# The second memory's keys and values as products of two fp32r parts, with the low parts made on GpSimd

## The chip, the cores and the metric

The kernel runs on one core of one Trainium2 chip. The metric is the device time of one execution in microseconds (us). Three runs of the kernel before gave 2437.41 us (median), from 2435.37 to 2440.38. TensorE is called PE in the rows, VectorE DVE, ScalarE ACT, GpSimd POOL, and SyncE, which issues most transfers, SP.

## The reference, cut to what matters

256 tokens of width 1024 pass through a three-layer stack (two layers of the first block, one of the second), in fp32 throughout. The change touches layer 1 of the first block, in which a Conformer convolution is followed by a cross attention to a memory of 256 rows:

```
def conformer_conv(xn, pw1_w, pw1_b, dw_w, dw_b, ln_g, ln_b, pw2_w, pw2_b):
    a, g = jnp.split(xn @ pw1_w + pw1_b, 2, axis=-1)
    h = a * jax.nn.sigmoid(g)
    h = depthwise_conv(h, dw_w) + dw_b           # 31 taps, 1024 channels
    h = jax.nn.silu(layernorm(h, ln_g, ln_b))
    return h @ pw2_w + pw2_b

def cross_attn(xn, mem, norm_mem, wq, wkv, wo):
    q = (xn @ wq).reshape(b, s, 4, 256)
    k, v = jnp.split(rmsnorm(mem, norm_mem) @ wkv, 2, axis=-1)
    ...
```

The keys and values depend on the memory alone and not on the tokens, so `rmsnorm(mem) @ wkv` (256x1024 by 1024x2048) can be computed at any time before the attention. There are three memories, one for each layer: A, B and C. The second one, B, is that of layer 1.

## The kernel before

**Units and panels.** The dense products are cut into units of 512 output columns (`UNITS`, lines 107 to 158). A unit's weights are one panel of 128 x 8 x 512 floats (2 MB), which SP loads into one of three slots of a ring (line 458). A unit is computed in one of two ways (`project`, line 603):

- *As parts.* The panel is taken in two halves of 128x2048. ScalarE rounds a half to fp32r into `w_high` (`highs`, line 1231), then VectorE subtracts that from the source and writes the rest, also in fp32r, to `w_low` (`lows`, line 1595). There are three buffers of each (`SPLITS`). The inputs are split likewise: ScalarE writes `XT_high` (`columns_high`, line 1220), VectorE `XT_low` (`columns_low`, line 1586). TensorE computes each product as three matmuls, high by high, low by high and high by low (`product`, lines 679 to 681).
- *Plain.* TensorE multiplies the fp32 panel itself (lines 617 and 622). ScalarE and VectorE each copy half of the fp32 input columns to `XT` (`columns`, lines 1206 and 1571).

Nearly all units go as parts. Plain are the four of memory B (`Bk0`, `Bk1`: keys; `Bv0`, `Bv1`: values) and `mix0`, `mix1`, `pw2_0`, `pw2_1`.

**Counters.** `parts_high` counts the halves that ScalarE has rounded, `parts_split` those whose low part is written, `parts_read` those that TensorE has read. A half waits for the one three places before it to be read. SP loads a panel when the panel three places before it is released: by `parts_split` for a unit as parts, and when TensorE is done with it for a plain one.

**The order around the change** is written out by hand on each engine. TensorE computes the gates and values of the convolution's gated input (`gate0`, `value0`, `gate1`, `value1`, as parts), transposes the normalised memory (line 666), computes `Bk0`, `Bk1`, `Bv0`, `Bv1`, does the convolution of 2 of the 8 blocks of 128 channels with 62 diagonal matrices (line 841), sums the channels for the layer norm (lines 846 and 850), computes `pw2_0` and `pw2_1` (line 622) and goes on to the attention. ScalarE evicts the four units (lines 1242 and 1237), and after the last it makes the 62 diagonals in six buffers (line 1383). VectorE, once it has copied its half of the memory's columns, does the convolution of the other 6 blocks: 6 instructions of line 1853 and 180 of line 1855, 31 rounds of 6, each `CO = HC * weight + CO` over 128x256 floats, with `HC`, `CO` and the weight in SBUF. The first channel sums wait for both parts of the convolution. GpSimd issues transfers only: after it has asked for memory B (line 537) it waits until the bias row of `pw2` has been used (line 1868).

**The same thing once before.** Memory A in layer 0 has the same four units, as parts already: its highs and columns are ScalarE's, its lows are VectorE's, between other work.

Of the kernel before, what the change touches and what calls it, by code (L numbers as in the profile page):

```python
# [14 lines left out]
F32 = mybir.dt.float32  # L15
F32R = mybir.dt.float32r
I32 = mybir.dt.int32
ALU = mybir.AluOpType
# [95 lines left out]


def _memory_units(tag, layer, wk, wv, v0):
    src = "memory" if tag == "B" else "x"
    for j in range(2):
        _unit(f"{tag}k{j}", wk, j * PANEL, PANEL, True, src, layer)
    for j in range(2):  # L120
        _unit(f"{tag}v{j}", wv, v0 + j * PANEL, PANEL, False, src, layer)
# [75 lines left out]
def program(nc, ins, const_in, out):  # L197
    ctx = ExitStack()
    with ctx:
# [5 lines left out]
        def S(name):  # L205
            if name not in sems:
                sems[name] = ctx.enter_context(nc.semaphore(name))
            return sems[name]

        ring = sb("ring", [P, 7, HALF])  # L210
        w_high = sb("w_high", [P, SPLITS, HALF], F32R)
        w_low = sb("w_low", [P, SPLITS, HALF], F32R)
        parts = sb("parts", [P, 3 * KC * P], F32R)
# [5 lines left out]
        XS = sb("XS", [P, HALVES, D])  # L219
# [154 lines left out]
        def half_source(q):  # L374


            i, kind, half, n = pieces_split[q]
            if kind == "rows":
                return ring[:, 2 * slot(i), :]
            if kind == "features":  # L380
                return slot_kn(slot(i))[:, 4 * half:4 * half + 4, 0:n]
            if q in range(ffn_at, ffn_at + 3 * FFN_TURNS):
                return slot_kn(slot(i)).rearrange("p k (g n) -> p k g n", g=2)[:, :, :, half * P:(half + 1) * P]
            return slot_kn(slot(i))[:, :, half * T:(half + 1) * T]

        def half_tile(q, parts):

            t, (_, kind, _, n) = parts[:, q % SPLITS, :], pieces_split[q]
            if kind == "rows":
                return t  # L390
            if kind == "features":
                return t.rearrange("p (k n) -> p k n", n=PANEL)[:, :, 0:n]
            if q in range(ffn_at, ffn_at + 3 * FFN_TURNS):
                return t.rearrange("p (k g n) -> p k g n", g=2, n=P)
            return t.rearrange("p (k n) -> p k n", n=T)

        def halves_to(name, more=0):

            return split_at[UNIT[name]] + 2 + more
# [123 lines left out]
        def _(pool):  # L523
# [11 lines left out]
            def memory(turns, name):  # L535
                pool.wait_ge(S("turned"), 4 * turns)
                pool.dma_start(XS[:, :, :], ins[name][0].rearrange("(a p) d -> p a d", p=P)).then_inc(S("memory_loaded"), 16)
# [3 lines left out]
            def row(b, src):  # L541

                if loads[b]:
                    pool.wait_ge(S(f"brow{b}_used"), loads[b])
                loads[b] += 1
                pool.dma_start(brow[:, b, :], src).then_inc(S(f"brow{b}_loaded"), 16)
# [27 lines left out]
            pool.wait_ge(S("pool_mixed"), 1)  # L574
            row(0, ins["od_pw2_b"][0].partition_broadcast(P))
            memory(5, "mem")
            row(0, ins["od_norm_moe"][0].partition_broadcast(P))
            row(0, ins["ln_in_g_2"].partition_broadcast(P))
            expert_rows(1, XS, "xs_ready", 8)
# [19 lines left out]
        def _(pe):  # L599
# [54 lines left out]
            def turn(src, ready, n, parts=True):  # L654

                pe.wait_ge(S(ready), n)
                if seen["act"]:
                    pe.wait_ge(S("columns_by_act"), seen["act"])
                    pe.wait_ge(S("columns_by_vector"), seen["vector"])

                seen["act"] += 4 if parts else 2
                seen["vector"] += 4 if parts else 2
                for kc in range(KC):
                    for tc in range(HALVES):
                        o = kc % 2 * T + tc * P
                        last = nc.tensor.transpose(ps[:, 4 + kc // 2, o:o + P], src[:, tc, kc * P:(kc + 1) * P], IDENT)  # L666
                    if kc % 2:
                        last.then_inc(S("turned"), 1)

            def columns_ready():  # L670

                pe.wait_ge(S("columns_by_act"), seen["act"])
                pe.wait_ge(S("columns_by_vector"), seen["vector"])
# [8 lines left out]

            def memory_projections(tag, ready, value):

                turn(XS, ready, value, parts=(tag != "B"))
                if tag == "B":
                    columns_ready()
                for name in ("k0", "k1", "v0", "v1"):
                    project(tag + name, first=(name == "k0"))

# [470 lines left out]
        def _(act):  # L1161
# [35 lines left out]
            def columns(dst, gain, banks=(4, 5)):  # L1197

                n_["turn"] += 1
                act.wait_ge(S("turned"), 4 * n_["turn"] - 2)  # L1200
                for kc in range(4):
                    src = ps[:, 4 + kc // 2, kc % 2 * T:kc % 2 * T + T]
                    if gain is None:
                        last = A(dst[:, kc, :], src, ACT.Copy)
                    else:
                        last = A(dst[:, kc, :], src, ACT.Copy, scale=vec(gain[0], gain[1] + kc))
                    if kc % 2:
                        last.then_inc(S("columns_by_act"), 1)

            def columns_high(gain):  # L1210

                n_["turn"] += 1
                for kc in range(KC):
                    if kc % 2 == 0:
                        act.wait_ge(S("turned"), 4 * n_["turn"] - 3 + kc // 2)
                    src = ps[:, 4 + kc // 2, kc % 2 * T:kc % 2 * T + T]
                    if gain is None:
                        last = A(XT_high[:, kc, :], src, ACT.Copy)
                    else:
                        last = A(XT_high[:, kc, :], src, ACT.Copy, scale=vec(gain[0], gain[1] + kc))  # L1220
                    if kc % 2:
                        last.then_inc(S("columns_by_act"), 1)

            def highs(end):

                while n_["high"] < end:
                    q = n_["high"]
                    wait_panel(act, pieces_split[q][0])
                    if q >= SPLITS:
                        act.wait_ge(S("parts_read"), q - SPLITS + 1)  # L1230
                    A(half_tile(q, w_high), half_source(q), ACT.Copy).then_inc(S("parts_high"), 1)  # L1231
                    n_["high"] += 1
# [26 lines left out]
                rms(XS, "memory_loaded", 16 * ("ABC".index(tag) + 1), junk=w_(10240, HALVES, D), shared=False)  # L1259

            def memory_projections(tag, gain):
                if tag == "B":
                    columns(XT, gain)
                else:
                    highs(halves_to(f"{tag}k0", 1))
                    columns_high(gain)
                    highs(halves_to(f"{tag}k1"))
                take_columns(f"{tag}k0", KT[:, 0:4, :])
                if tag == "C":
                    layer_norm()  # L1270
                if tag != "B":
                    highs(halves_to(f"{tag}v0"))
                take_columns(f"{tag}k1", KT[:, 4:8, :])
                if tag != "B":
                    highs(halves_to(f"{tag}v1"))
                for j in range(2):
                    take(f"{tag}v{j}", VM[:, :, j * 512:(j + 1) * 512])

# [251 lines left out]
        def _(dve):  # L1530
# [31 lines left out]
            def columns(dst, gain):  # L1562
                n_["turn"] += 1
                n_["act"] += 2
                dve.wait_ge(S("turned"), 4 * n_["turn"])
                for kc in range(4, 8):
                    src = ps[:, 4 + kc // 2, kc % 2 * T:kc % 2 * T + T]
                    if gain is None:
                        last = V.tensor_copy(dst[:, kc, :], src)
                    else:  # L1570
                        last = V.tensor_scalar(dst[:, kc, :], src, vec(gain[0], gain[1] + kc), None, MUL)
                    if kc % 2:
                        last.then_inc(S("columns_by_vector"), 1)
# [57 lines left out]
            def row(b):  # L1631
                n_[f"b{b}"] += 1
                dve.wait_ge(S(f"brow{b}_loaded"), 16 * n_[f"b{b}"])
                return brow[:, b, :]
# [197 lines left out]
            for j in range(2):  # L1832
# [12 lines left out]
                if j == 0:  # L1845
                    rms(XS, XS, EPS)
                    lows(halves_to("value1"))
            columns(XT, ("xa_norm_mem", 8))
            for k in range(CONV):
                for kc in range(KC - TAPS_ON_PE):  # L1850
                    wv = vec("od_dw_w", KC * k + kc)
# [12 lines left out]
            V.tensor_scalar(VAR, ps[:, 5, 0:T], 1.0 / D, EPS, MUL, ADD).then_inc(S("variance_ready"), 1)  # L1864
            rsqrt(RST, STD)
            V.tensor_tensor(CO, CO, rep(RST), MUL).then_inc(S("standard"), 1)
            b = row(0)
            use_row(0, V.tensor_tensor(H[:, :, :], H[:, :, :], b.rearrange("p (a n) -> p a n", a=1).broadcast_to([P, 2, D]), ADD))
            for j in range(2):
# [384 lines left out]
```

## Time and profile before

| | before |
|---|---|
| profiled execution, us | 2436.28 |
| its span, us | 2434.5 |
| PE busy, us (share) | 2240.4 (92%) |
| DVE busy | 1733.0 (71%) |
| ACT busy | 1368.5 (56%) |
| POOL busy | 54.3 (2%) |
| mean granted TensorE clock | 0.953 |
| DMA, mean | 249 GB/s |

Times in the rows are counted from the span's start. The execution takes 1.78 us more than the span. The stretch of the change, from the transposes of memory B to the start of `pw2_0`, is 481 to 593 us: 4.6% of the span. A granted clock of 1.00 is 2.4 GHz and 0.50 is 1.2 GHz.

### The profile page before, as it was taken

What the parts mean: (1) busy time and instruction counts of PE and PEld (TensorE: products, weight loads), DVE (VectorE), ACT (ScalarE), POOL (GpSimd) and SP (SyncE); (2) the same over time, 40 slices, a digit from 0 to 9 for tenths busy, and PEclk for the clock granted to TensorE, in tenths of its full rate; (3) what the DMA queues carried; (4) which work ended last, traced back from release to release, by engine and by line L of the source; (5) the groups of instructions that cost most, each with busy time, mean ns of one, the idle gap of its engine ahead of it and who ended that gap; (6) DMA issues with size and microseconds to landing.
All of it is one profiled execution on the core that took longest, in us unless ns stands there. A gap on an engine that the chain in (4) does not pass through costs nothing.

```text
span 2434.5 us, 30265 instructions
## 1 busy us (share of the span) xinstructions
PE 2240.4 (92%) x11513; PEld 1892.4 (78%) x11513; DVE 1733.0 (71%) x1575; ACT 1368.5 (56%) x1191; POOL 54.3 (2%) x62
## 2 busy tenths in 40 slices
PE   7998999897878999999999999999699788699996
PEld 7867998865767888888888888888589677688884
DVE  4544544594437898989888888888646545489986
ACT  4333333414316777777777777777455243377774
POOL 2000000000000000000000000000000000000000
PEclk9999999998978999999999999999889899599998
DMA  9432555440337999999999999999533252399993
GB/s 307 150 140 87 189 175 190 156 138 9 104 147 277 370 351 379 350 375 352 369 354 371 355 368 350 377 354 369 191 115 109 87 181 96 121 352 354 352 352 125
DMA packets 271691, 605.54 MB, mean 249 GB/s; under 512 B 9232, under 2 KB 34016, under 8 KB 271616
## 3 DMA queue, kind: packets, MB, share of 16 engines
q1 hardware_dynamic: 265360, 583.39, 67.2%
q0 software_dynamic: 6256, 21.11, 2.6%
q8 instruction: 53, 0.87, 0.2%
q14 instruction: 22, 0.18, 0.0%
HBM read 601.31 MB, written 3.15 MB: 248 GB/s over the span
## 4 chain that ended last, share of the span: by engine, by line
PE 80%; DVE 5%; ACT 4%; issue 2%; ACTq 0%; POOL 0%; DVEq 0%
PE ps L679 22%; PE ps L681 22%; PE ps L680 22%; PE ps L622 2%; DVE w_low L1988 1%; PE ps L939 1%; PE ps L617 1%; PE ps L841 1%; ACT w_high L1444 1%; PE ps L868 1%; PE ps L666 1%; DVE w_low L1595 1%; PE ps L924 1%; PE ps L697 1%; ACT L1444 1%
## 5 line engine op out<-in xcount | busy, mean ns | idle before, releaser
L1988 DVE TENSOR_TENSOR w_low<-ring,w_high 128x2048 fp32r<-128x2048 f32 x432 | 983.8, 2290 | 143.7 <-ACT w_high L1444 142.7
L1444 ACT ACTIVATE w_high<-ring 128x2048 fp32r<-128x2048 f32 x432 | 824.3, 1917 | 179.3 <-PE ps L681 179.1
L680 PE MATMUL ps<-w_high,parts 128*128 128x512 f32 x2088 | 813.8, 390 | 0.0
L679 PE MATMUL ps<-w_high,parts 128*128 128x512 f32 x1816 | 723.0, 398 | 29.6 <-DVE w_low L1988 14.9
L681 PE MATMUL ps<-w_low,parts 128*128 128x512 f32 x1816 | 711.4, 392 | 0.0
L680 PEld LDWEIGHTS ps<-w_high,parts 128*128 128x128 f32 x2088 | 395.3, 189 | 77.1
L679 PEld LDWEIGHTS ps<-w_high,parts 128*128 128x128 f32 x1816 | 343.0, 189 | 109.3 <-issue 23.9
L681 PEld LDWEIGHTS ps<-w_low,parts 128*128 128x128 f32 x1816 | 342.6, 189 | 73.9
L1595 DVE TENSOR_TENSOR w_low<-ring,w_high 128x2048 fp32r<-128x2048 f32 (+2 forms) x109 | 243.5, 2250 | 114.8 <-ACT w_high L1231 107.8
L1231 ACT ACTIVATE w_high<-ring 128x2048 fp32r<-128x2048 f32 (+2 forms) x109 | 204.1, 1882 | 200.8 <-PE ps L681 156.0
L679 PE MATMUL ps<-XT_high,w_high 128*128 128x256 f32 x1024 | 294.7, 288 | 20.7 <-DVE parts L1584 8.9
L680 PE MATMUL ps<-XT_high,w_low 128*128 128x256 f32 x1024 | 292.1, 285 | 0.0
L681 PE MATMUL ps<-parts,w_high 128*128 128x256 f32 x1024 | 291.9, 285 | 0.0
L679 PEld LDWEIGHTS ps<-XT_high,w_high 128*128 128x128 f32 x1024 | 199.2, 195 | 23.4 <-issue 17.1
L680 PEld LDWEIGHTS ps<-XT_high,w_low 128*128 128x128 f32 x1024 | 199.3, 195 | 0.5
L681 PEld LDWEIGHTS ps<-parts,w_high 128*128 128x128 f32 x1024 | 198.9, 194 | 0.0
L679 PE MATMUL ps<-w_high,XT_high 128*128 128x512 f32 (+2 forms) x272 | 105.6, 388 | 0.0
L681 PE MATMUL ps<-w_low,XT_high 128*128 128x512 f32 (+2 forms) x272 | 103.4, 380 | 0.0
L1430 ACT ACTIVATE parts<-ps 128x512 fp32r<-128x512 f32 x72 | 43.2, 600 | 94.7 <-PE ps L939 94.7
L666 PE MATMUL ps<-const,XS 128*128 128x128 f32 x160 | 30.8, 373 | 48.8 <-DVE XS L1553 26.7
L1855 DVE SCALAR_TENSOR_TENSOR work<-work,cols 128x256 f32<-128x256 f32 x180 | 73.9, 481 | 1.1
L1426 ACT ACTIVATE work<-ps 128x512 f32<-128x512 f32 x72 | 43.1, 598 | 49.9 <-PE ps L681 49.8
(364 smaller groups left out, 1754.6 us busy)
## 6 DMA issues: line engine op xcount, KB each, us to landing
ring<-in_od_moe_gu SPq DMA_DIRECT2D x224, 1024.0 KB, 7.1
ring<-in_od_moe_down SPq DMA_DIRECT2D x112, 1024.0 KB, 7.0
ring<-in_w SPq DMA_DIRECT2D x96, 1024.0 KB, 7.1
ring<-in_ev_ffn_gu SPq DMA_DIRECT2D x22, 1024.0 KB, 7.4
ring<-in_xa_wkv SPq DMA_DIRECT2D x8, 2048.0 KB, 8.8
ring<-in_od_pw_w SPq DMA_DIRECT2D x6, 2048.0 KB, 8.3
ring<-in_w_in SPq DMA_DIRECT2D x6, 2048.0 KB, 7.9
ring<-in_ev_ffn_down SPq DMA_DIRECT2D x11, 1024.0 KB, 5.1
```

The costliest lines, as they stand in the source:

```text
L622: last = mm(pair[:, tc, 0:n], x[:, kc, tc * P:(tc + 1) * P], w[:, kc, 0:n], start=(kc == 0), stop=(kc == KC - 1))
L666: last = nc.tensor.transpose(ps[:, 4 + kc // 2, o:o + P], src[:, tc, kc * P:(kc + 1) * P], IDENT)
L679: mm(out_, xh, wh, start=start, stop=False)
L680: mm(out_, xl, wh, start=False, stop=False)
L681: return mm(out_, xh, wl, start=False, stop=stop)
L1231: A(half_tile(q, w_high), half_source(q), ACT.Copy).then_inc(S("parts_high"), 1)
L1426: A(SG, ps[:, 0, :], ACT.Silu).then_inc(moe_sem(k, "silu"), 1)
L1430: A(h_high[:, :, :], ps[:, 4, :].rearrange("p (k t) -> p k t", t=P), ACT.Copy)\
L1444: A(w_high[:, j % SPLITS, :], ring[:, j % NS, :], ACT.Copy).then_inc(moe_sem(k, "high"), 1)
L1595: V.tensor_tensor(half_tile(q, w_low), half_source(q), half_tile(q, w_high).bitcast(F32), SUB)\
L1855: last = V.scalar_tensor_tensor(CO[:, kc, :], HC[:, kc, k:k + T], wv, CO[:, kc, :], MUL, ADD)
L1988: V.tensor_tensor(w_low[:, j % SPLITS, :], ring[:, j % NS, :], w_high[:, j % SPLITS, :].bitcast(F32), SUB)\
```

## The change

Memory B's four units become units as parts. ScalarE's and TensorE's programs are then those of memories A and C. VectorE writes `XT_low` instead of its half of `XT`, counts the eight low parts of B as done (`n_["halves"]`) and goes straight to the convolution. GpSimd writes these eight low parts, each when `parts_high` says that ScalarE has its high part; ahead of them stands the last low part of VectorE's own (of `value1`). VectorE waits for the eighth before it uses the `pw2` bias row.

```diff
 def _memory_units(tag, layer, wk, wv, v0):
-    src = "memory" if tag == "B" else "x"
+    src = "x"
...
             memory(5, "mem")
+            pool.wait_ge(S("parts_split"), halves_to("Bk0", -2))
+            for q in range(halves_to("Bk0", -2), halves_to("Bv1")):
+                pool.wait_ge(S("parts_high"), q + 1)
+                nc.gpsimd.tensor_tensor(half_tile(q, w_low), half_source(q), half_tile(q, w_high).bitcast(F32), ALU.subtract)\
+                    .then_inc(S("parts_split"), 1)
             row(0, ins["od_norm_moe"][0].partition_broadcast(P))
...
             def memory_projections(tag, ready, value):        # TensorE
-                turn(XS, ready, value, parts=(tag != "B"))
-                if tag == "B":
-                    columns_ready()
+                turn(XS, ready, value)
...
             def memory_projections(tag, gain):                # ScalarE
-                if tag == "B":
-                    columns(XT, gain)
-                else:
-                    highs(halves_to(f"{tag}k0", 1))
-                    columns_high(gain)
-                    highs(halves_to(f"{tag}k1"))
+                highs(halves_to(f"{tag}k0", 1))
+                columns_high(gain)
+                highs(halves_to(f"{tag}k1"))
                 take_columns(f"{tag}k0", KT[:, 0:4, :])
                 if tag == "C":
                     layer_norm()
-                if tag != "B":
-                    highs(halves_to(f"{tag}v0"))
+                highs(halves_to(f"{tag}v0"))
                 take_columns(f"{tag}k1", KT[:, 4:8, :])
-                if tag != "B":
-                    highs(halves_to(f"{tag}v1"))
+                highs(halves_to(f"{tag}v1"))
...
-            columns(XT, ("xa_norm_mem", 8))                   # VectorE
+            columns_low(("xa_norm_mem", 8))
+            n_["halves"] = halves_to("Bv1")
             for k in range(CONV):
...
             V.tensor_tensor(CO, CO, rep(RST), MUL).then_inc(S("standard"), 1)
+            dve.wait_ge(S("parts_split"), halves_to("Bv1"))
             b = row(0)
```

`half_source(q)` is the q-th half in the ring, `half_tile(q, w_low)` its place in buffer q % 3. Each of GpSimd's subtractions is over 128x2048 floats and has both its inputs in SBUF.

## Rows read from the trace of the kernel before

**Rows 1.** Page, part 4: shares of the span on the chain that ended last.

```profile
PE 80%; DVE 5%; ACT 4%; issue 2%; ACTq 0%; POOL 0%; DVEq 0%
```

**Rows 2.** Chain that ended last in order of time, 400 to 700 us (start, us, what).

```profile
485.00 27.87 PE ps L617 x128
512.86 27.48 PE ps L622 x64
...
541.82 27.03 PE ps L841 x124
568.88 0.85 ACT work L1388 x2
569.77 3.73 PE ps L846 x16
573.53 0.44 DVE work L1859
...
576.32 2.30 DVE work L1862
578.66 5.54 PE ps L850 x16
...
593.34 30.75 PE ps L622 x64
```

**Rows 3.** Timeline of VectorE, 420 to 680 us (start, us, instruction, [idle before <-releaser]).

```profile
433.37 3.42 DVE L1586 SCALAR_TENSOR_TENSOR parts<-ps,cols,XT_high 128x256 fp32r<-128x256 f32 x8
...
466.15 2.29 DVE L1595 TENSOR_TENSOR w_low<-ring,w_high 128x2048 fp32r<-128x2048 f32 x1 [1.42 <-ACT w_high L1231]
481.43 1.66 DVE L1840 SCALAR_TENSOR_TENSOR work<-ps,cols,work 128x256 f32<-128x256 f32 x4 [12.98 <-PE ps L681]
483.24 1.66 DVE L1571 TENSOR_SCALAR ring<-ps,cols 128x256 f32<-128x256 f32 x4
484.81 2.02 DVE L1853 TENSOR_SCALAR work<-work,cols 128x256 f32<-128x256 f32 x6
486.87 74.96 DVE L1855 SCALAR_TENSOR_TENSOR work<-work,cols 128x256 f32<-128x256 f32 x180
573.53 0.43 DVE L1859 TENSOR_SCALAR work<-ps 128x256 f32<-128x256 f32 x1 [11.70 <-PE ps L846]
```

**Rows 4.** Timeline of ScalarE, 420 to 680 us.

```profile
432.48 3.40 ACT L1220 ACTIVATE XT_high<-ps,cols 128x256 fp32r<-128x256 f32 x8 [2.87 <-PE ps L666]
...
541.29 25.40 ACT L1383 ACTIVATE work<-const,cols 128x128 f32<-128x128 f32 x62
```

**Rows 5.** Timeline of ScalarE, 66 to 118 us: memory A, as parts.

```profile
67.27 1.91 ACT L1231 ACTIVATE w_high<-ring 128x2048 fp32r<-128x2048 f32 x1 [3.84 <-PE ps L681]
69.09 3.02 ACT L1220 ACTIVATE XT_high<-ps,cols 128x256 fp32r<-128x256 f32 x8
77.97 1.92 ACT L1231 ACTIVATE w_high<-ring 128x2048 fp32r<-128x2048 f32 x1 [5.87 <-PE ps L681]
...
84.60 1.91 ACT L1231 ACTIVATE w_high<-ring 128x2048 fp32r<-128x2048 f32 x1
89.49 1.92 ACT L1231 ACTIVATE w_high<-ring 128x2048 fp32r<-128x2048 f32 x1 [2.99 <-PE ps L681]
...
96.11 1.91 ACT L1231 ACTIVATE w_high<-ring 128x2048 fp32r<-128x2048 f32 x1
101.05 1.92 ACT L1231 ACTIVATE w_high<-ring 128x2048 fp32r<-128x2048 f32 x1 [3.02 <-PE ps L681]
...
116.98 1.02 ACT L1237 ACTIVATE work<-ps 128x1024 f32<-128x1024 f32 x1 [9.85 <-PE ps L681]
```

**Rows 6.** Timeline of VectorE, 60 to 135 us: memory A's low input columns.

```profile
70.74 3.22 DVE L1586 SCALAR_TENSOR_TENSOR parts<-ps,cols,XT_high 128x256 fp32r<-128x256 f32 x8
```

**Rows 7.** Stretches (us; each engine busy; granted clock; DMA).

```profile
573.60:576.00 2.40, 0.00 (x0) 0.00 (x0) 2.37 (x2) 0.00 (x0) 0.00 (x0) 0.90 0.00 0
576.00:579.00 3.00, 0.34 (x1) 0.34 (x2) 2.58 (x2) 0.00 (x0) 0.00 (x0) 0.50 0.00 0
```

## The prediction

> **What bounds the kernel now.** I read the chain of waits by engine first: 80% of the span is TensorE [rows 1]. That is a mean over stages, so I went to the chain in order of time around the change [rows 2] to see whether TensorE's work is what each moment waits for. From 485.0 to 540.3 us it is: the four plain units of memory B take 27.87 + 27.48 us, then the 62 diagonals' matmuls (27.0 us), the eviction of their result (0.85 us), and at 569.77 the channel sums begin. Next, VectorE's own timeline shows who is second [rows 3]: its half of the convolution starts at 484.81 and the last of 180 instructions ends at 486.87 + 74.96 = 561.8. The sums need both halves, so VectorE is early by only 569.8 - 561.8 = 8.0 us. This is the most that a faster TensorE can gain here, whatever it saves in the four units, and the change also touches VectorE's start.
>
> **TensorE's part: 9.9 us earlier.** Memory A does the same four units as parts, at the same full clock, so its rows give a timetable. There the low columns start at 70.74 [rows 6] and the last unit is evicted at 116.98 [rows 5]: 46.2 us later. In B the start follows from the order of the engines. TensorE is done with `value1` at 481.4, when VectorE's wait for it ends [rows 3]; ScalarE then has a high half to write first, 69.09 - 67.27 = 1.8 us [rows 5], so its columns start at 483.2; VectorE's low columns follow 433.37 - 432.48 = 0.9 us behind [rows 3, 4], at 484.1. The last unit is thus done at 484.1 + 46.2 = 530.4 against 540.3 (512.86 + 27.48 [rows 2]): 9.9 us gained, if the low halves are there in time. The eviction of the units and the 62 diagonals (one ScalarE instruction per 0.41 us [rows 4], which sets the pace of TensorE's 27.0 us) keep their length, so the diagonals' matmuls end at 568.9 - 9.9 = 559.0 and their eviction at 559.9.
>
> **VectorE's part, if nothing disturbs it: 2.6 us later.** It loses four copies (1.66 us from 483.24) and gets eight low columns, 3.4 us from 484.1 [rows 3]. The convolution starts at 487.5, not 484.8, and ends at 561.8 + 2.7 = 564.5. VectorE is then last, after TensorE's 559.9: the sums start at 564.5 instead of 569.8, 5.3 us earlier. The other 4.6 us of TensorE's gain turn into idle time.
>
> **GpSimd's part: is it in time?** With the shift of 484.1 - 70.7 = 413.4 us, ScalarE writes B's halves 3 to 7 (counted from 0) from 491.4, 498.0, 502.9, 509.5 and 514.4, 1.9 us each [rows 5]. No row shows GpSimd computing, so the price of one subtraction over 128x2048 has to be bounded. Below stands VectorE's own 2.29 us for the same operands [rows 3]. For the upper end I take an engine that takes two inputs and an output one after the other, three passes, 6.9 us. My value is two passes, 4.6 us, which is a choice: I do not expect it to read both inputs at once as VectorE does. The Trainium skill, "GPSIMD Engine Reference", section "Elementwise — side-by-side cycle accounting", gives 4497 ns for a two-input operation of this size; by it the sum below would come out 0.4 us lower. No run here shows it yet. The high halves 5 and 7 waited for TensorE to have read halves 2 and 4, so TensorE reaches half 3 at 502.9 and half 5 at 514.4, and ends at 530.4, which is 5.3 us for each of the last three. The low halves would be ready at high + 1.9 + 4.6: half 3 at 497.9 (wanted 502.9), 4 at 504.5 (509.1), 5 at 509.4 (514.4), 6 at 516.0 (519.8), 7 at 520.9 (525.1). A subtraction can take 3.8 us more than I assume before TensorE waits. The weights' transfers are released by the low halves and come earlier than before, and the rows that GpSimd asks for behind the subtractions are first wanted after VectorE's bias row at 589, so I price both at nothing. If GpSimd were late there, the `od_norm_moe` row would have the whole attention to land in. VectorE's new wait for the eighth half costs nothing either: it stands ahead of the bias row, some 70 us after half 7's high part.
>
> **What I expect to decide: the two engines getting into each other's way.** The convolution's 180 instructions have two tensors in SBUF as inputs, and so have the subtractions. In this trace nothing on GpSimd computes beside VectorE, so the cost lies between nothing and the full length of every overlapping subtraction. Halves 0 and 1 are split before VectorE has its convolution to do. Half 2 gets its high part in 481.4 to 483.3, and its subtraction (to 487.9) lies beside the low columns, which have PSUM as one input, and 0.4 us into the convolution. Halves 3 to 7 lie wholly within it. If VectorE stands still for each, it loses 5 x 4.6 + 0.4 = 23.3 us, and the convolution ends at 564.5 + 23.3 = 587.8, 18.0 us behind the old start of the sums.
>
> The Trainium skill, "SBUF — State Buffer", section "Who interferes with whom", says just this: a VectorE instruction with two SBUF inputs contends with a GpSimd instruction that reads SBUF, one holds the shared ports for its whole length and the other is blocked. No row of the trace before can show whether it is so.
>
> **The clock.** TensorE has nothing to do from 559 on. After the first sums it stood idle in 573.6 to 576 and by 576 to 579 its granted clock was 0.50 [rows 7]; the second sums, equal in work to the first, then took 5.54 us against 3.73 [rows 2]. With any idle time of 5 us or more ahead of the first sums I let these cost 5.54 too: 1.8 us. The second sums and `pw2` have the same idle time ahead of them as before.
>
> **The sum.** +18.0 + 1.8 = +19.8 us. Everything behind the sums is a chain of the same work and moves as a whole. The profiled execution took 2436.28 us (span 2434.5 and 1.78 around it), 1.1 below the runs' median of 2437.41; 2436.3 + 19.8 = 2456.1, so I forecast 2456 us. With a subtraction of 2.29 us the stall is 11.5 us and the time 2444; with 6.9 us it is 34.9 and 2468.
>
> **The rivals.**
>
> *They don't disturb each other.* VectorE streams through ports of its own, the convolution ends at 564.5, and the time is 2436.3 - 5.3 + 1.8 = 2432.8 us; without the clock's 1.8 it is 2431.0, and this is the floor. This holds if VectorE's stall stays below 3.5 us in all, 0.7 us for each of five subtractions; above that the change loses. For it speaks that each instruction of line 1855 is short, 0.42 us, with only 256 elements; against it the two SBUF inputs on both sides.
>
> *They share word by word.* At VectorE's rate of 2048 elements in 2.29 us, 256 elements stream for 0.29 us of the 0.42 from start to start (74.96 / 180 [rows 3]). Shared in turn these become 0.58, the slot 0.70 us; GpSimd advances at 59% and takes 7.8 us for a subtraction, in which VectorE does 11 instructions and not 19: 3.2 us lost, 16.0 in five. The convolution ends at 580.5, and TensorE, late by some 8 us for the halves 4 to 7, still ends its units before 540. 10.7 + 1.8 = +12.5: 2449 us.
>
> *VectorE always goes first.* GpSimd only advances in the 0.13 us between two instructions, 30%, so a subtraction takes 15 us. Of five from 493.3 on, 4.7 are done when the convolution ends at 564.5; the last is ready at 566.0, TensorE ends at 571.3, and the 29.4 us from there to the sums (540.3 to 569.8 [rows 2]) give 600.7, +31 us: 2467 us. The bound has then moved to GpSimd. The weak point of this rival is that VectorE waits for itself after each round of six, which would let the other in.
>
> **How the numbers follow.** Whole blocking 0.50, no disturbance 0.22, sharing 0.15, VectorE first 0.06, and 0.07 for what I don't see. Blocking and its duration's bounds spread from 2444 to 2468, most of it in 2449 to 2462, which is this case's own range. To leave out no more than 2 in 10 the range must take in the undisturbed case, so it goes from 2432 to 2462. A change of under 0.2%, 4.9 us, can't be told from none. Slower by more: 0.50 + 0.15 + 0.06 and 0.02 of the rest, 0.73. Within: 0.18, nearly all of it the undisturbed case with its 3.5 us. Faster by more needs the floor: 0.09.
>
> **What would show it.** On GpSimd: eight subtractions, the last five from about 493, 500, 505, 511 and 516, of some 4.6 us. On VectorE: line 1855 starts at 489.5 or so, and if blocked, it has five gaps or five single instructions of about 4.6 us beside them, all others staying at 0.48; if shared, dozens of longer ones; and its sum is 75 + 23 us. On TensorE: lines 679 to 681 in place of 617 and 622, done by 530.4, the diagonals by 559, then idle until about 588 at a falling clock, and `pw2` from about 613. I am wrong if line 1855's stretch stays near 75 us, if a subtraction is nearer to 2.3 or over 8 us, or if TensorE waits for low halves.

## The result, and the profile after

The change makes the kernel slower: 2445.51 us (median of seven runs, 2443.66 to 2448.36) against 2437.41 us (seven runs, 2433.11 to 2440.38), a ratio of 1.0034, 95% interval [1.0023, 1.0045], +8.1 us. The forecast was 2456 us, +19.8. The profiled execution took 2448.36 us with a span of 2446.6, 12.1 us more span than before.

The stage of the change came out nearly as worked out. The after-trace runs 1.8 us late before it reaches the change at all (VectorE gets the last value at 483.26, not 481.43 [rows 3]), so its times are read with 1.8 us off. The mark at 119 us, long before any changed instruction, is already 1.9 us late. First VectorE's timeline, in the columns of [rows 3]:

```profile
483.26 1.66 DVE L1838 SCALAR_TENSOR_TENSOR work<-ps,cols,work 128x256 f32<-128x256 f32 x4 [12.98 <-PE ps L686]
486.00 3.23 DVE L1584 SCALAR_TENSOR_TENSOR parts<-ps,cols,XT_high 128x256 fp32r<-128x256 f32 x8 [1.07 <-ACT XT_high L1223]
489.14 2.52 DVE L1852 TENSOR_SCALAR work<-work,cols 128x256 f32<-128x256 f32 x6
491.70 96.81 DVE L1854 SCALAR_TENSOR_TENSOR work<-work,cols 128x256 f32<-128x256 f32 x180
595.25 0.42 DVE L1858 TENSOR_SCALAR work<-ps 128x256 f32<-128x256 f32 x1 [6.75 <-PE ps L849]
```

The 180 instructions take 96.81 us and not 74.96: 21.85 us more for the same work. GpSimd's timeline shows what lies beside them:

```profile
475.27 9.19 POOL L580 TENSOR_TENSOR w_low<-ring,w_high 128x2048 fp32r<-128x2048 f32 x2 [37.42 <-ACT w_high L1234]
485.31 4.58 POOL L580 TENSOR_TENSOR w_low<-ring,w_high 128x2048 fp32r<-128x2048 f32 x1 [0.85 <-ACT w_high L1234]
495.23 4.72 POOL L580 TENSOR_TENSOR w_low<-ring,w_high 128x2048 fp32r<-128x2048 f32 x1 [5.34 <-ACT w_high L1234]
501.84 4.63 POOL L580 TENSOR_TENSOR w_low<-ring,w_high 128x2048 fp32r<-128x2048 f32 x1 [1.89 <-ACT w_high L1234]
506.75 4.87 POOL L580 TENSOR_TENSOR w_low<-ring,w_high 128x2048 fp32r<-128x2048 f32 x1 [0.28 <-ACT w_high L1234]
513.36 9.46 POOL L580 TENSOR_TENSOR w_low<-ring,w_high 128x2048 fp32r<-128x2048 f32 x2 [1.75 <-ACT w_high L1234]
```

Five subtractions lie within the convolution. The chain of waits, in order of time, tells the rounds of six instructions apart:

```profile
491.70 2.48 DVE work L1854 x6
494.20 6.84 DVE work L1854 x6
501.06 11.24 DVE work L1854 x6
512.33 11.18 DVE work L1854 x6
523.54 2.48 DVE work L1854 x6
...
588.71 6.52 PE ps L849 x16
595.71 2.30 DVE work L1860
...
600.39 5.83 PE ps L853 x16
...
615.35 29.20 PE ps L627 x64
```

A round takes 2.48 us. One that meets the first subtraction takes 4.4 more, the next two, with two each, 8.8 and 8.7 more; from 523.54, when GpSimd is done, every round is 2.48 again. The longest single instruction of line 1854 is 4.885 us, against a median of 0.481. VectorE stands still while GpSimd subtracts: 21.85 us over five subtractions is 4.4 us for each, of the 4.6 to 4.9 that one takes.

The 486.00 row shows a case beside it that isn't held up. The low input columns read one tensor from PSUM and one from SBUF and write SBUF, and the third subtraction (485.31 to 489.89) lies over all eight; they take 3.23 us, against 3.22 for the same eight in [rows 6] with GpSimd idle.

In TensorE's place [rows 2], ScalarE's rows show the units done by 532.24 and the taps by 560.75 (530.4 and 558.9 without the 1.8 us):

```profile
532.24 1.02 ACT L1240 ACTIVATE work<-ps 128x1024 f32<-128x1024 f32 x1 [9.85 <-PE ps L686]
533.16 25.40 ACT L1381 ACTIVATE work<-const,cols 128x128 f32<-128x128 f32 x62
560.75 0.84 ACT L1386 ACTIVATE work<-ps,cols 128x256 f32<-128x256 f32 x2 [2.19 <-PE ps L844]
```

TensorE then stands idle for 28 us, until VectorE is done:

```profile
588.71 6.51 PE L849 MATMUL ps<-work,const 128*128 128x256 f32 x16 [28.00 <-DVEq L1856]
```

The time that is missing from the forecast is given back far behind. GpSimd's transfers are good marks, as each is asked for when another engine is done with a step. Its timeline of before:

```profile
591.71 0.55 POOL L546 DMA_DIRECT2D brow<-in_od_norm_moe  x1 [155.71 <-DVE H L1868]
...
1740.64 0.57 POOL L546 DMA_DIRECT2D brow<-in_ln_in_b  x1 [81.30 <-DVE H L2031]
...
1834.17 0.53 POOL L546 DMA_DIRECT2D brow<-in_ln_b  x1 [84.80 <-DVE work L2095]
1915.12 0.71 POOL L537 DMA_DIRECT2D XS<-in_mem  x1 [80.41 <-PE ps L666]
```

and of after:

```profile
613.72 0.58 POOL L546 DMA_DIRECT2D brow<-in_od_norm_moe  x1 [90.90 <-DVE H L1868]
...
1759.21 0.58 POOL L546 DMA_DIRECT2D brow<-in_ln_in_b  x1 [80.26 <-DVE H L2031]
...
1846.62 0.53 POOL L546 DMA_DIRECT2D brow<-in_ln_b  x1 [78.68 <-DVE work L2095]
1924.98 0.71 POOL L537 DMA_DIRECT2D XS<-in_mem  x1 [77.83 <-PE ps L671]
```

Late by 22.0 us behind the convolution (20.2 without the early 1.8), by 18.6 at the start of the second block, by 12.4 and 9.9 within its mixer, and by 12.1 at the end. The largest piece, 6.2 us, lies in the mixer, where the instructions are the same. Stretches show why: the granted clock is the third number from the right. Before:

```profile
1780.00:1795.00 15.00, 15.00 (x47) 10.65 (x47) 4.33 (x11) 0.65 (x3) 0.00 (x0) 0.54 0.02 8
```

and the same place in after, 18.6 us later:

```profile
1798.60:1813.60 15.00, 15.00 (x86) 12.11 (x86) 9.08 (x17) 5.54 (x19) 0.00 (x0) 1.00 0.07 17
```

TensorE has a wait of 1.2 us just ahead in both. Before, the granted clock of the 15 us is 0.54, nearly all of them at 1.2 GHz, and they hold 47 matmuls; after, it is 1.00, 2.4 GHz, and they hold 86.

The sum can now be closed. From +20.2 us behind the convolution, 9.9 are given back: +10.3 at the end of the trace. The medians differ by 8.1; the other 2.2 us are the two profiled executions' own places, before's 1.1 us below its median and after's 2.9 above, less the early 1.8.

### The profile page after: what moved, and what is told of

Its sections match the earlier page's. It is cut to its first block, busy times and chain, and to the rows that moved or that the text cites. A ratio compares the mean times of both kernels' runs of the same rounds, so it can differ in the third digit from the quotient of the medians.

```text
span 2446.6 us, 30492 instructions
## 1 busy us (share of the span) xinstructions
PE 2224.1 (91%) x11609; PEld 1894.2 (77%) x11609; DVE 1756.8 (72%) x1579; ACT 1384.6 (57%) x1203; POOL 91.9 (4%) x70
## 4 chain that ended last, share of the span: by engine, by line
PE 75%; DVE 9%; ACT 4%; issue 2%; ACTq 0%; POOL 0%; DVEq 0%
PE ps L684 22%; PE ps L686 22%; PE ps L685 22%; DVE work L1854 4%; DVE w_low L1988 1%; PE ps L942 1%; PE ps L627 1%; ACT w_high L1442 1%; PE ps L871 1%; PE ps L671 1%; DVE w_low L1593 1%; PE ps L700 1%; ACT L1442 1%; PE ps L927 1%; PE ps L720 1%
## 5 line engine op out<-in xcount | busy, mean ns | idle before, releaser
L685 PE MATMUL ps<-w_high,parts 128*128 128x512 f32 (+2 forms) x2120 | 825.3, 389 | 0.0
L684 PE MATMUL ps<-w_high,parts 128*128 128x512 f32 x1816 | 722.9, 398 | 29.8 <-DVE w_low L1988 14.8
L1234 ACT ACTIVATE w_high<-ring 128x2048 fp32r<-128x2048 f32 (+2 forms) x117 | 219.4, 1884 | 220.0 <-PE ps L686 177.0
L684 PE MATMUL ps<-XT_high,w_high 128*128 128x256 f32 x1088 | 315.8, 290 | 22.7 <-DVE parts L1582 8.9
L685 PE MATMUL ps<-XT_high,w_low 128*128 128x256 f32 x1088 | 313.1, 288 | 0.0
L686 PE MATMUL ps<-parts,w_high 128*128 128x256 f32 x1088 | 312.7, 287 | 0.0
L684 PEld LDWEIGHTS ps<-XT_high,w_high 128*128 128x128 f32 x1088 | 214.6, 197 | 25.5 <-issue 19.2
L685 PEld LDWEIGHTS ps<-XT_high,w_low 128*128 128x128 f32 x1088 | 214.5, 197 | 0.5
L1854 DVE SCALAR_TENSOR_TENSOR work<-work,cols 128x256 f32<-128x256 f32 x180 | 95.8, 602 | 1.1
L558 POOL DMA_INDIRECT work<-row_store,rows_at x12 | 27.0, 2254 | 1244.5 <-DVE rows_at L1931 1244.5
```

Of the source, the lines that this page charges most:

```text
L558: pool.indirect_dma_start(expert_in[:, :], None, row_store[k], bass.IndirectOffsetOnAxis(rows_at[:, 0:1], 0))\
L684: mm(out_, xh, wh, start=start, stop=False)
L685: mm(out_, xl, wh, start=False, stop=False)
L686: return mm(out_, xh, wl, start=False, stop=stop)
L1854: last = V.scalar_tensor_tensor(CO[:, kc, :], HC[:, kc, k:k + T], wv, CO[:, kc, :], MUL, ADD)
```

## The experiments

Two questions: what holds VectorE up, and where some 10 us of the delay went. The marks of all traces, in us later than before, stand in one table below.

**Accumulate the convolution in PSUM.** The changed kernel; the accumulator of the convolution, one of the two inputs of each instruction and its output, now lies in PSUM. Only the last round of six still writes SBUF. TensorE's two blocks share bank 4.

```diff
+                    acc = ps[:, 5 + kc // 2, kc % 2 * T:kc % 2 * T + T]
...
-                        last = V.scalar_tensor_tensor(CO[:, kc, :], HC[:, kc, k:k + T], wv, CO[:, kc, :], MUL, ADD)
+                        last = V.scalar_tensor_tensor(CO[:, kc, :] if k == CONV - 1 else acc, HC[:, kc, k:k + T], wv, acc, MUL, ADD)
```

> After, with the convolution of VectorE accumulating in PSUM: each of its instructions has one SBUF tensor and one PSUM tensor as input. Blocking theory (VectorE stands still only where both engines read two tensors from SBUF): the 180 instructions take about 75 us and none is over 0.6 us, the subtractions stay at 4.6 us, the channel sums start about 22 us earlier than in after, and the time is 2433 us, if everything behind moves as a whole, or 2437 at most. Rival (any GpSimd computation slows VectorE, or sharing is by time and not by input): the stretch stays at 97 us and the time at 2445. Rival on the clock: if the median is above 2437, what is behind the sums does not move one for one.

2431.12 us, ratio to before 0.9975 [0.9964, 0.9985]. VectorE's and GpSimd's timelines:

```profile
491.20 71.98 DVE L1856 SCALAR_TENSOR_TENSOR ps<-work,cols,ps 128x256 f32<-128x256 f32 x174
563.22 2.44 DVE L1856 SCALAR_TENSOR_TENSOR work<-work,cols,ps 128x256 f32<-128x256 f32 x6
571.28 0.42 DVE L1860 TENSOR_SCALAR work<-ps 128x256 f32<-128x256 f32 x1 [5.62 <-PE ps L849]
```

```profile
495.76 4.64 POOL L580 TENSOR_TENSOR w_low<-ring,w_high 128x2048 fp32r<-128x2048 f32 x1 [6.74 <-ACT w_high L1234]
502.36 4.64 POOL L580 TENSOR_TENSOR w_low<-ring,w_high 128x2048 fp32r<-128x2048 f32 x1 [1.96 <-ACT w_high L1234]
```

180 instructions in 74.5 us beside five subtractions at the same places (two of them shown): VectorE isn't held up, and none of the 180 takes over 0.49 us. The rival, that any computation on GpSimd slows it, is out. The run moves the output as well as an input, so by itself it can't say which of the two counts. The low input columns above can: they write SBUF with one input from there, and aren't held up. This kernel is what the undisturbed case of the prediction described, at 2432.8 us.

**Let GpSimd only write.**

```diff
-                nc.gpsimd.tensor_tensor(half_tile(q, w_low), half_source(q), half_tile(q, w_high).bitcast(F32), ALU.subtract)\
+                nc.gpsimd.memset(w_low[:, q % SPLITS, :].bitcast(F32), 0.0)\
```

> After, with GpSimd's subtractions replaced by fills of the same 128x2048 buffers with zero (the low parts are left out). GpSimd then reads nothing. Blocking by reads: line 1854's stretch is 75 us, as in before, time 2433. Rival, blocking by any use of the ports: each fill of 1 to 5 us stops VectorE for its length, five of them, 5 to 22 us, time 2437 to 2445.

The low parts are left out. 2432.24 us, 0.9983 [0.9974, 0.9992]. The convolution is at its old length beside fills of 1.8 us:

```profile
493.37 74.98 DVE L1854 SCALAR_TENSOR_TENSOR work<-work,cols 128x256 f32<-128x256 f32 x180
```

**Let GpSimd read one input.** `tensor_scalar(half_tile(q, w_low), half_source(q), 0.001, None, ALU.mult)` in place of the subtraction, which leaves the low parts out as well.

> After, with GpSimd scaling the source by a constant into the low part's buffer in place of the subtraction (the low parts are then wrong in value): it reads one tensor and not two. Blocking for GpSimd's whole instruction: line 1854's stretch is 75 us plus five times one such instruction; if that takes 2.3 us, 86.5 us, if 4.6, again 97. If the blocking needs two inputs on GpSimd's side as well, it is 75 us.

One run, 2444.04 us. Neither number of the expectation:

```profile
495.90 5.55 POOL L580 TENSOR_SCALAR w_low<-ring 128x2048 fp32r<-128x2048 f32 x1 [5.26 <-ACT w_high L1234]
502.51 11.10 POOL L580 TENSOR_SCALAR w_low<-ring 128x2048 fp32r<-128x2048 f32 x2 [1.06 <-ACT w_high L1234]
```

```profile
488.40 4.00 DVE L1852 TENSOR_SCALAR work<-work,cols 128x256 f32<-128x256 f32 x6
492.44 91.88 DVE L1854 SCALAR_TENSOR_TENSOR work<-work,cols 128x256 f32<-128x256 f32 x180
```

One input is enough for the blocking. But the instruction takes 5.5 us, longer than the subtraction, and holds VectorE up for only (91.88 - 74.98) / 5 = 3.4 us. Why these differ stays open. On who is held up, the three runs agree with the Trainium skill, "SBUF — State Buffer", section "Who interferes with whom": a VectorE instruction with two SBUF inputs contends with GpSimd reading, not with GpSimd only writing, and one with at most one SBUF input doesn't contend, outside the 2-port modes, which the page says `tensor_scalar` can enter. On how long, they agree in part. The page has the ports held for the whole instruction: the subtraction took 4.4 us of VectorE for its 4.7, but this one 3.4 for its 5.5.

**VectorE makes the low parts.** Eight subtractions of 2.29 us, three ahead of the convolution, five between its rounds 3 to 9, none on GpSimd.

```diff
...
+            lows(halves_to("Bk0"))
             columns_low(("xa_norm_mem", 8))
-            n_["halves"] = halves_to("Bv1")
+            lows(halves_to("Bk0", 1))
             for k in range(CONV):
+                lows({3: halves_to("Bk1"), 5: halves_to("Bv0", -1), 6: halves_to("Bv0"), 8: halves_to("Bv1", -1),
+                      9: halves_to("Bv1")}.get(k, 0))
```

> After, with the eight low parts made by VectorE again: three before the convolution and five between its rounds, 2.29 us each. Then VectorE carries 11.5 us more in the convolution in place of the 21.8 us it stands still in after, and about 2 us more ahead of it. The sums start 8 to 9 us earlier than in after and some 8 us later than in before. Theory A: 2437 + 8 + 2 = 2447 against after's 2456 by the same theory; theory B: nearly the same as after, 2440 to 2446, since the giving back depends on when the second block comes.

2451.7 us, 1.0059 [1.0044, 1.0074], over both numbers of the expectation (2447, and 2440 to 2446). Part of this was a term too small: the three subtractions ahead of the convolution push its 180 instructions back by 4.5 us against after, and not by about 2.

```profile
496.24 4.97 DVE L1852 SCALAR_TENSOR_TENSOR work<-work,cols 128x256 f32<-128x256 f32 x12
```

The mark behind the convolution still comes at 606.4, 7.3 us ahead of after's, and yet the median is 6.2 us above after's. It cannot be read without the second question.

**The same delay without GpSimd.** Kernel before, with 60 instructions of the convolution's kind behind the convolution, into a scratch place:

```diff
+            for i in range(60):
+                last = V.scalar_tensor_tensor(w_(10240, KC, T)[:, i % 6, :], HC[:, i % 6, 0:T], vec("od_dw_w", 0), CO[:, i % 6, :], MUL, ADD)
+                if i % 6 == 5:
+                    step(last)
```

> Before, with 60 more instructions of the convolution's kind on VectorE behind it, into a scratch place: 25.0 us more on VectorE, 8.0 of them hidden, so the channel sums start 17.0 us later, as they do in after. No GpSimd work, and the four units plain. Theory A (what is behind moves as a whole): 2437 + 17 + 1.8 = 2456. Theory B (part of any delay here is given back in the second block, where the granted clock comes out otherwise): the sums and the expert stage are 17 to 19 us later, but the time is 2443 to 2449, and the stretch 1780 to 1795 us of before, at a clock of 0.54, is at 1.00.

2446.17 us, 1.0047 [1.0033, 1.0061]. The mark behind the convolution is 19.8 us late, the end 9.8. Its trace gives time back in after's places and by after's amounts (table), so the giving back needs neither GpSimd's work nor the four units as parts. The five runs lie far apart: 2445.46, 2446.06 (the traced one), 2446.17, 2450.59 and 2452.99, with mean granted clocks of 0.954, 0.955, 0.955, 0.952 and 0.951.

With 48:

> Before, with 48 instead of 60 more instructions of the convolution's kind: 20.0 us, 8.0 hidden, the sums 12.0 us later, near the 13.4 us of vector_lows. Theory B1 (the clock in the second block takes one of two courses, and which one hangs on how late the block comes): the course of before, the clock falls to 0.50 behind the wait near 1776 + shift, nothing is given back, and the time is 2436.3 + 14 = 2450, later than delay60's 2446 in spite of 5 us less delay. Rival B2 (it hangs on the kernel's form, on what the added work is): the same course as delay60, and the time is 2446 - 5 = 2441.

2449.75 us, 1.0056 [1.0039, 1.0073]. The median is 3.6 us above delay60's with 5 us less work, but the two sets of runs overlap (2446.71 to 2451.17 here, 2445.46 to 2452.99 there), so the times don't order the two kernels. The traces say more: this one is 10.7 us late behind the convolution and 10.4 at the end; nothing is given back. With 96:

> Before, with 96 more instructions: 40.0 us, 8.0 hidden, the sums 32.0 us later, 34 us at the start of pw2. Course of before all the way: 2436.3 + 34 = 2470. Course of delay60 and after: 8 to 10 us less, 2460 to 2462. If the time is below 2455, a third thing gives time back in proportion to the delay.

2469.57 us, 1.0136 [1.0119, 1.0153], 33.2 us late and 33.0 at the end.

**Is it how late the second half comes?** Two runs for that, `vector_lows` with 12 such instructions and the changed kernel with 30.

> vector_lows with 12 more instructions of the convolution's kind on VectorE, 5.0 us that lie on the path. The row asked for at 591.7 in before would be 19.7 us late instead of 14.7, within the 17.8 to 22.0 us at which three kernels have taken the second course of the clock. Theory B1 (which course is taken hangs on how late the second half comes): it takes the second course, and is some 3 to 5 us faster than vector_lows in spite of the added work, 2446 to 2449. Rival B2 (the course hangs on the form of the work): the course of vector_lows, 2456 to 2457.

2453.28 us, 1.0066 [1.0051, 1.0082]. Not as B1 had it: at 19.7 us late, between kernels that give back 10 us at 17.8 and 19.8, it goes like before (the mixer gives nothing back up to 1834, then 2.6).

> After, with 30 more instructions of the convolution's kind behind the convolution, 12.5 us on the path: that row is 34 us late, near delay96's 33.2. Theory B1: the first course, as delay96, 2469 to 2472, so that 12.5 us of work cost 24 or more. Rival B2 (after's form takes the second course whenever it comes) and theory C (any delay from 15 us on gives back 8): 2445 + 12.5 = 2458.

2466.78 us, 1.0121 [1.0106, 1.0137]: 12.5 us of added work cost 21.3. Here B1's number was right and its rivals' 2458 wrong: in these traces neither after's form nor a long delay brings the giving back by itself.

**The changed kernel again.**

> The changed kernel again, for its trace. If the course of the clock belongs to how late the second block comes, it is that of the first trace of after: 1.00 in the 15 us behind the wait that is at 1776 in before, end 12 us behind before. If it is chance, one trace in a few shows before's course, and then the time is some 6 us longer.

2447.65 us, the same course as in its first trace.

The marks, in us later than in before (its times in the heading), with the length of the first channel sums and of `pw2`:

| kernel | first sums | pw2 | 435.3 | 591.7 | 702.8 | 1740.6 | 1834.2 | 1915.1 | 2424.9 |
|---|---|---|---|---|---|---|---|---|---|
| before | 3.73 | 30.75 | 0 | 0 | 0 | 0 | 0 | 0 | 0 |
| psum_acc | 5.39 | 30.66 | 1.1 | -2.4 | -2.6 | -2.5 | -2.6 | -2.6 | -2.7 |
| psum_moved | 3.71 | 30.55 | 1.3 | -5.4 | -5.7 | -5.7 | -5.8 | -5.8 | -5.8 |
| write_only | 5.75 | 30.70 | 4.0 | 0.7 | 0.6 | 0.7 | 0.6 | -1.9 | -1.6 |
| delay48 | 5.41 | 30.61 | -2.7 | 10.7 | 10.5 | 10.5 | 10.4 | 10.4 | 10.4 |
| vector_lows | 5.86 | 30.76 | 1.3 | 14.7 | 14.7 | 14.8 | 14.7 | 14.7 | 14.6 |
| vector_lows12 | 5.16 | 30.54 | 2.2 | 19.7 | 19.4 | 19.5 | 19.4 | 16.8 | 17.1 |
| delay96 | 5.66 | 30.67 | -0.6 | 33.2 | 33.1 | 33.0 | 33.0 | 33.0 | 33.0 |
| after30 | 5.42 | 30.61 | 2.3 | 33.3 | 33.1 | 33.2 | 33.1 | 33.1 | 33.0 |
| one_input | 6.47 | 29.19 | 1.2 | 17.8 | 17.0 | 14.3 | 8.2 | 5.6 | 7.8 |
| delay60 | 6.46 | 29.18 | -0.4 | 19.8 | 19.1 | 16.2 | 10.2 | 7.6 | 9.8 |
| after | 6.52 | 29.20 | 1.8 | 22.0 | 21.3 | 18.6 | 12.4 | 9.9 | 12.1 |
| after again | 6.53 | 29.20 | 1.2 | 21.4 | 20.6 | 17.9 | 11.8 | 9.2 | 11.4 |

The traces fall into two courses with nothing between: the first sums take at most 5.9 us and `pw2` over 30.5, or the sums take 6.5 and `pw2` 29.2. All of the second kind, and none of the first, then give back 3.4 to 3.6 us up to 1740 and 6.0 to 6.2 in the mixer up to 1834; the end is 10 us nearer. Two of the first kind, write_only and vector_lows12, give back 2.5 and 2.6 us later, between 1834 and 1915. The course is thus visible at the first idle time of TensorE behind the convolution, 1200 us ahead of its largest effect. Both are courses of the granted clock: it rises and falls at other moments of the same work. In the 15 us behind the wait (1780 to 1795 in before, the same work in the others) it is 0.54 in all nine traces of the first kind and 1.00 in all four of the second. Between before and after it also differs in `pw2` (0.90 and 0.95), at 730 to 745 us of before (0.61 and 0.77) and at 1717 to 1732 (0.91 and 1.00), and these are the stretches in which its first 3.4 us, up to 1740, are given back.

What picks a course is not settled. It isn't the delay by size, nor the kernel's form. It isn't the length of TensorE's idle time ahead of the first sums either: that was 18.2, 23.1 and 28.0 us (twice) in the second kind, and 0.7 to 16.9, 21.8, 33.2 and 40.5 in the first. And it may not be the kernel at all. There is one trace of each kernel and two of after, so whether executions of one kernel differ in their course was not tested; delay60's runs, 7.5 us apart, leave room for it.

**A version that beats both.** In `psum_acc` TensorE waits 4.6 us for VectorE. Six taps of block 5 go to TensorE, into the free bank of `Bv0`, with one addition:

```diff
-                for kc in range(KC - TAPS_ON_PE):
+                for kc in range(KC - TAPS_ON_PE - (k >= CONV - MOVED)):
...
+            dve.wait_ge(S("diagonal_used"), TAPS_ON_PE * CONV + MOVED)
+            step(V.tensor_tensor(CO[:, 5, :], CO[:, 5, :], PAIRS[UNIT["Bv0"] % 2][:, 0, 0:T], ADD))
```

> psum_acc, and six of the 31 taps of one channel block moved from VectorE to TensorE, whose eviction of the taps comes some 5 us before VectorE's end in psum_acc: VectorE does 6 x 0.41 = 2.5 us less and one addition more (0.4), TensorE 6 x 0.44 = 2.6 us more. The sums start about 2 us earlier than in psum_acc, and without the idle time ahead of them they take 3.73 and not 5.5 us: 3.8 us less in all, 2427 us. If the clock falls all the same: 2 us less, 2429.

2430.76 us, 0.997 [0.9958, 0.9982], 6.9 us under the median of before's runs beside it, and above both numbers of the expectation (2427 and 2429). TensorE's idle time ahead of the sums is down to 0.7 us, and the sums start 1.1 us earlier than in psum_acc, not 2 (chain, in order of time):

```profile
564.79 3.71 PE ps L856 x16
```

The sums take 3.71 us again, as in before, and the marks are 3 us earlier than in psum_acc from 591.7 to the end. The two medians, 0.4 us apart with runs spread over 5 us and more, do not tell the two kernels apart; that the step gains is shown by one trace of each alone.

## Why the prediction was wrong

- **TensorE's part** held. 9.9 us of gain were worked out from memory A's rows; without the early 1.8 us the last unit is evicted at 530.4, as written, and the taps end at 558.9 (559.0 written).
- **VectorE's start** held: 489.14, or 487.3 (487.5 written).
- **GpSimd's price** held: 4.6 to 4.9 us for a subtraction, chosen at 4.6 between bounds of 2.29 and 6.9. It was in time: the last low half was ready before 523, wanted at 527 in the trace's time. The margin was worked out wrongly, though. I let each subtraction be 3.8 us longer by itself, but they queue: the five from 493.3 have to be done by 525.1, so TensorE would have waited from 6.4 us each on, 1.8 more than assumed. At 4.6 to 4.9 this had no effect. Two small sums are off as well: with 4.5 us for a subtraction the total comes out 0.6 us lower, not 0.4, and with 6.9 half 2 reaches 2.7 us into the convolution and not 0.4, which makes the stall 37.2 us and not 34.9.
- **The blocking** held: 21.85 us in the 180 instructions and 0.5 in the six ahead of them, 22.3 in all, 23.3 written. The sharing rival and the one with VectorE first are out: one instruction took 4.885 us and the median stayed at 0.481, and a subtraction took under 5 us, not 7.8 or 15. The undisturbed one is out by the length of the 180.
- **The clock at the first sums** was mis-sized: 6.52 us, not 5.54, and the second 5.83. `pw2`, held to be as before, came down by 1.55 from [rows 2]. Up to the mark behind the convolution the sum was +19.8 and the trace has +20.2.
- **The step that failed** is "Everything behind the sums is a chain of the same work and moves as a whole". The work is the same, its duration isn't: in after 9.9 us are given back between 591.7 and the end, 6.2 of them in the mixer, where the granted clock is 1.00 in a stretch that had 0.54. The sum put this at nothing. delay60 shows the same giving back with no part of the change in it, and after30 that it is gone with 12.5 us more. Why the clock takes this course stays open. Had the changed kernel gone the way of vector_lows or after30, it would have come out near 2445.5 + 9.9 = 2455 us, an estimate from the table. I had taken TensorE's clock into account only at the idle time that the change makes, and not at those that it merely shifts.
- The range held the time by luck. It was drawn wide to take in the undisturbed case, and 2445.5 lies near its middle, where the price of blocking was right and a term outside the sum took half of it away. The forecast itself was over twice the true change.

A part of the difference between the profiled executions, the 1.8 us ahead of the change, is of neither kernel's making: the other traces of this study stand between -2.7 and +4.0 us at the 435.3 mark, some with identical code up to it.

## What to carry to other kernels

Before work is moved to GpSimd beside VectorE, look at what both read. Here it cost nothing beside `scalar_tensor_tensor` with one of its two tensors in PSUM, or when GpSimd only wrote, and almost its whole length beside `scalar_tensor_tensor` with both in SBUF. One SBUF input is no safe sign alone: `tensor_scalar` from SBUF to SBUF was held up too (below). Before giving up such a split, see whether VectorE's accumulator can live in PSUM: here that alone turned +8 us into -5. The slack of one engine in the trace of before (8.0 us here, between VectorE's and TensorE's ends) bounds the gain before any price is worked out.

In this kernel, which TensorE bounds with short idle times here and there, a delay of d us was not always d us at the end. It was 10 us less in four traces, and vector_lows, 7.3 us ahead of after behind the convolution, came out 6.2 us slower. A verdict on a change of under 10 us wants a second kernel with a pure delay beside it, and the traces' marks compared all the way to the end.

## What the runs showed that I had not expected

- Two courses of the granted clock for the same work, 10 us apart at the end, the same one in both traces of the changed kernel, and ordered neither by how late the work comes nor by how long TensorE had stood idle.
- A one-input `tensor_scalar` on GpSimd over 128x2048 took 5.5 us, more than the two-input subtraction's 4.6, and blocked VectorE for 3.4 us of it.
- The six `tensor_scalar` instructions ahead of the convolution, with a single SBUF tensor as input, took 4.00 us in one_input and 2.52 in after, where GpSimd's third instruction runs into them, against 2.02 [rows 3]: they are held up too. So the number of SBUF inputs alone doesn't decide it.
- A VectorE accumulation in PSUM cost no more than in SBUF: 180 instructions in 74.5 us against 75.0, though the six `tensor_scalar` ahead of them, with their output in PSUM, took 2.78 us against 2.02.
